# Two-block transformer on one core: compression inputs in two places, gates' activations grouped, products beside the first attention steps

## The chip, the cores and the metric

The kernel runs on one NeuronCore of a Trainium2 chip. The metric is the device time of one execution in microseconds (us). The engines named are TensorE (PE, with its weight loads as PEld), VectorE (DVE), ScalarE (ACT), GpSimd (POOL) and the queue that issues the DMAs (SP).

## What is computed

Two transformer blocks over 512 tokens of width 1024, all in float32. The first has forget-gate attention and differential attention side by side and then a mixture of 32 experts. The change lies mostly in the second block's mixer, which in the reference, cut to what matters, is:

```python
def compress_blocks(kv, pos, w1, w2):           # for the keys and for the values
    blocks = jnp.concatenate([c[:, :, :-1], c[:, :, 1:]], axis=3) + pos    # 31 windows of 32 tokens
    hid = jax.nn.silu(blocks.reshape(B, H, -1, CMP_BLOCK * DH) @ w1)       # (2048 -> 256)
    return hid @ w2                                                        # (256 -> 64)

# sparse attention, 8 heads in 2 groups, 4 query blocks of 128: over the compressed keys,
# over the selected blocks and over a window; the three are gated and added
o = gc[..., 0:1] * o_c + gc[..., 1:2] * o_s + gc[..., 2:3] * o_w

qk = silu(causal_depthwise_conv(concatenate([mq, mk]), conv_w, conv_b))    # width 4
hm = mlstm_chunkwise(mq, mk, mv, mi + bias, log_sigmoid(mf + bias))        # 4 heads
y = concatenate([y_nsa, sigmoid(mo) * normed(hm)]) @ w_out
```

## The kernel before

It is one program with a list of instructions for each engine, written stage by stage; every wait is on a semaphore that another engine's finished instruction raises. An engine takes its instructions strictly in the order written. There is no planner: the order is made by hand with generators. Dense products are done as three matmuls on split float32 (a high and a low part): ScalarE casts the high part of a weight piece (`se_lead_to`, L601), VectorE subtracts the low part (`ve_lead_to`, L590). All matmuls are recorded under the helper line L525.

The stages around the change, in order:

- **Projection** (`pe_project_nsa`, `ve_project_nsa`, `se_project_nsa`, from L2365). TensorE makes gate rows, keys and values, and then for kv = 0 (keys) and 1 (values) the compression: for two halves of the output over 16 slices each (64 recorded matmuls), with a stationary operand of 128 columns and 62 moving columns (`cmp`), a Silu on ScalarE into `hc` and a second product (`cmp2`). VectorE adds the positions to the windows and writes them to `XC` (`windows(kv)`, L2423). `XC` and `hc` have one place each, so the windows of kv = 1 wait for the `cmp` products of kv = 0, and stand behind the copy of the first `cmp2` (L2446). The stage ends with small transposes (`gat`, `mcol`) and an exponential (L2485).
- **Sparse attention** (`pe_nsa`, `ve_nsa`, `se_nsa`, from L2552): 36 units, for each of 4 head pairs first the compressed scores (branch 0, all four query blocks) and then 8 units of rising width (query block i, two branches). Step s does, per engine: TensorE the scores of unit s (A), the transposes of unit s-2 (C), beats, the values of unit s-3 (E); VectorE the normalisation of unit s-1 (N), bias and maxima of unit s (B), beats; ScalarE the copies of transposed scores (C), the exponential of unit s (B), beats. A **beat** is half a chunk (12 products of 512 columns) of the convolution's projection `mqk`, or a chunk (24 of 256) of the values' projection `mv`, with what the other engines do for it (`beside`, L648). `nsa_beats` (L2523) spreads 16 beats evenly over 36 steps: the first at step 2, then 4, 6, 8, 11, 13, 15, 17, 20, 22 and so on. The convolution c (`se_conv`, L2491, and `ve_conv`) copies its chunk to `cv` on ScalarE, and VectorE applies four taps (L2515, L2517). From c = 1 on, ScalarE puts the Silu of c-1 in front of that copy; the Silu of c = 3 stands at the first chunk of `mv`, in front of the next cast. Each Silu needs another activation table than the exponentials beside it.
- **mLSTM** (`pe_ml`, `ve_ml`, `se_ml`, from L2764): 16 units. For each head TensorE spreads a row over 128 partitions (`pe_row`, L1005): the stationary operand is 128 columns of a selector, loaded by DMA, which picks row h. ScalarE copies it (L1015), GpSimd masks it (L1021), ScalarE takes exponentials (L2834, L2835), VectorE multiplies with the scores. Beats make the output gates `og` in four chunks, each with a Sigmoid in its own place (`se_ogate`, L2809). TensorE enters the stage when all engines have ended the one before and the selector is there; SP issues the selector's DMA after these ends (`sp_ml`, L2738).

The first block's forget-gate attention uses the same `pe_row` with 8 heads and a selector of its own.

## Time and profile before

| | us |
|---|---|
| median of 3 runs | 1991.56 (1991.16 to 1992.77) |
| the profiled execution | 1991.63 |
| its span | 1989.8 |
| TensorE busy | 1778.8 (89%) |
| VectorE busy | 741.1 (37%) |
| ScalarE busy | 641.7 (32%) |
| GpSimd busy | 171.7 (9%) |

The page of the profile puts 49% of the chain that ended last on TensorE and 19% on DMA; the latter is 18% weights of the experts. The projection's end lies at about 1092 to 1122 us of the span, the sparse attention from there to 1289.7, the mLSTM up to about 1376. A busy time says how long an engine had an instruction under way; the figure in brackets behind a row of the timeline is how long the engine stood idle before it, and for whom. PEclk is the granted share of TensorE's full clock.

### The profile page before, as it was taken

The numbers are of one execution on the slowest core, as the hardware profiler recorded it, in microseconds if no ns is written. First come the engines' busy times: TensorE is split into PE (matmuls) and PEld (weight loads), VectorE is DVE, ScalarE is ACT, GpSimd is POOL, SyncE is SP. The second block draws the span as 40 slices with busy tenths as digits, with TensorE's granted clock in tenths as the row PEclk, the third lists the DMA queues.
The fourth block names the chain that finished last, engine by engine and source line by source line (L and its number), as shares of the span: only waits on it lengthen the run. The fifth ranks groups of instructions, "written<-read, shape, count | busy, mean of one in ns | idle before, by whom it ended". The sixth has DMA issues, their size and how long they took to land.

```text
span 1989.8 us, 22296 instructions
## 1 busy us (share of the span) xinstructions
PE 1778.8 (89%) x9148; PEld 1271.7 (64%) x9148; DVE 741.1 (37%) x1551; ACT 641.7 (32%) x1079; POOL 171.7 (9%) x134
## 2 busy tenths in 40 slices
PE   7999899996898888888849877898999999999998
PEld 6878566885333333333348755766888788888886
DVE  4454443455111111211164455554463452232313
ACT  3433465423010100010044255464432452122223
POOL 1000000131111111111010000011010110000111
PEclk9999899997998989899969688996999999999999
DMA  7412100357799999999934111012241122322211
GB/s 265 146 45 83 43 22 22 112 201 285 272 398 415 413 409 401 410 405 413 386 133 159 43 61 62 15 50 96 85 162 50 54 95 85 117 74 106 86 62 43
DMA packets 78445, 337.60 MB, mean 170 GB/s; under 512 B 7892, under 2 KB 15700, under 8 KB 65409
## 3 DMA queue, kind: packets, MB, share of 16 engines
q1 hardware_dynamic: 73216, 327.70, 42.7%
q0 software_dynamic: 5120, 8.40, 1.3%
q8 instruction: 75, 1.23, 0.3%
q14 instruction: 34, 0.27, 0.0%
HBM read 327.69 MB, written 16.78 MB: 173 GB/s over the span
## 4 chain that ended last, share of the span: by engine, by line
PE 49%; DMA 19%; DVE 7%; ACT 4%; issue 2%; POOL 0%; SPq 0%; POOLq 0%; DVEq 0%; ACTq 0%
PE ps L525 47%; DMA otf<-in_w 18%; DVE splitr L590 1%; ACT splitr L601 1%; DVE arenaf L2662 1%; ACT arenaf L2709 1%; PE ps L2582 1%; DVE xf L2159 1%; PE ps L772 1%; DVE otf L2517 0%; DVE xf L2967 0%; ACT hr L792 0%; PE ps L936 0%; DVE arenaf L2680 0%; DMA yd<-junk,idx 0%
## 5 line engine op out<-in xcount | busy, mean ns | idle before, releaser
L525 PE MATMUL ps<-hr,splitr 128*128 128x512 f32 (+1 forms) x2784 | 587.9, 371 | 15.0 <-issue 5.7
L525 PEld LDWEIGHTS ps<-hr,splitr 128*128 128x128 f32 x2784 | 482.8, 196 | 98.5 <-issue 14.9
L525 PE MATMUL ps<-splitr,hr 128*128 128x512 f32 (+1 forms) x1488 | 278.8, 349 | 0.0
L525 PEld LDWEIGHTS ps<-splitr,hr 128*128 128x128 f32 x1488 | 240.0, 194 | 33.6 <-issue 1.4
L590 DVE TENSOR_TENSOR splitr<-ring,splitr 128x2048 fp32r<-128x2048 f32 x63 | 145.8, 2316 | 212.2 <-ACT splitr L601 212.1
L525 PE MATMUL ps<-ring,arenaf 128*64 128x512 f32 x352 | 175.5, 657 | 20.6 <-DMA ring<-in_w 20.6
L601 ACT CAST splitr<-ring 128x2048 fp32r<-128x2048 f32 x63 | 119.9, 1904 | 161.5 <-PE ps L525 157.8
L525 PE MATMUL ps<-arenaf 128*64 128x128 f32 (+10 forms) x770 | 122.0, 365 | 28.3 <-DVE cells L2662 9.4
L1906 DVE TENSOR_TENSOR arenaf<-arenaf,ps 64x512 f32<-64x512 f32 x32 | 21.8, 681 | 328.2 <-ACT arenaf L1901 328.2
L1901 ACT ACTIVATE arenaf<-ps 64x512 f32<-64x512 f32 x32 | 19.0, 593 | 325.4 <-PE ps L525 325.4
L590 DVE TENSOR_TENSOR splitr<-arenaf,splitr 128x2048 fp32r<-128x2048 f32 x29 | 69.5, 2397 | 129.5 <-ACT splitr L601 129.5
L525 PE MATMUL ps<-splitf,arenaf 128*64 128x512 f32 x320 | 81.2, 665 | 26.8 <-DMA splitf<-in_w 26.8
L525 PEld LDWEIGHTS ps<-arenaf 128*64 128x64 f32 (+3 forms) x770 | 68.7, 171 | 54.1 <-issue 31.0
L525 PE MATMUL ps<-otf,arenaf 128*64 128x512 f32 x176 | 83.5, 631 | 19.7 <-DMA otf<-in_w 19.7
L525 PEld LDWEIGHTS ps<-ring,arenaf 128*64 128x64 f32 x352 | 50.9, 150 | 67.7 <-issue 67.6
L525 PE MATMUL ps<-splitr,otr 128*128 128x512 f32 x384 | 89.7, 392 | 1.5 <-DVE arenaf L3367 1.2
L525 PE MATMUL ps<-hf,arenaf 128*64 128x512 f32 x160 | 83.2, 681 | 0.0
L525 PEld LDWEIGHTS ps<-splitr,otr 128*128 128x128 f32 x384 | 71.5, 188 | 16.9 <-DVE arenaf L3367 1.5
L525 PE MATMUL ps<-arenaf,tq 128*64 128x512 f32 x336 | 76.7, 598 | 0.0
L601 ACT CAST splitr<-arenaf 128x2048 fp32r<-128x2048 f32 x29 | 55.2, 1903 | 59.6 <-PE ps L525 59.6
L525 PEld LDWEIGHTS ps<-splitf,arenaf 128*64 128x64 f32 x320 | 27.0, 153 | 73.3 <-issue 73.2
L926 ACT ACTIVATE arenaf<-arenaf,cells 128x128 f32<-128x128 f32 (+3 forms) x64 | 36.0, 562 | 117.5 <-DVE cells L920 117.4
(365 smaller groups left out, 2000.0 us busy)
## 6 DMA issues: line engine op xcount, KB each, us to landing
ring<-in_w SPq DMA_DIRECT2D x22, 2048.0 KB, 35.7
arenaf<-in_w SPq DMA_DIRECT2D x22, 2048.0 KB, 40.1
splitf<-in_w SPq DMA_DIRECT2D x21, 2048.0 KB, 35.5
hf<-in_w SPq DMA_DIRECT2D x20, 2048.0 KB, 35.2
ring<-in_w_in SPq DMA_DIRECT2D x11, 2048.0 KB, 11.2
otf<-in_w SPq DMA_DIRECT2D x11, 2048.0 KB, 39.5
ring<-in_w_gate_up SPq DMA_DIRECT2D x6, 2048.0 KB, 7.8
arenaf<-in_w_in SPq DMA_DIRECT2D x4, 2048.0 KB, 14.6
```

The lines of the kernel that those rows point to most:

```text
L525: return te.matmul(out, lhsT, rhs, start=start, stop=stop)
L590: ve.tensor_tensor(lo, loaded(e)[:, ks, cs], hi.bitcast(F32), ALU.subtract).then_inc(*ve_done("weights low", ("low", n), *([("entry used", ...
L601: se.copy(hi, loaded(e)[:, ks, cs]).then_inc(*se_done("weights high", ("high", n)))
L772: it = te.transpose(ps[:, 128 * k:128 * k + 128], scaled(nm, t)[:, 128 * kk:128 * kk + 128], ident)
L926: se.activation(sc[:, 0:n], sc[:, 0:n], ACT.Exp, bias=cell[:, 3:4], accum_out=cell[:, 4:5]).then_inc(*se_done("powers", ("exp",) + key))
L1901: se.activation(GATE, bank("up", b)[CAP:2 * CAP, :], ACT.Silu).then_inc(*se_done("gates", ("silu", b)))
L1906: ve.tensor_tensor(HROW, GATE, bank("up", b)[0:CAP, :], ALU.mult).then_inc(*ve_done("hidden", ("hid", b), ("free", "up", b)))
L2159: vstep(ve.scalar_tensor_tensor(X3[:, t, :], G2[:, t, 1024 * k:1024 * k + 1024], W8[:, 4 * k + t, :], X3[:, t, :], ALU.mult, ALU.add), *([ ...
L2582: it = te.transpose(ps[:, 128 * m:128 * m + 128], sc[k][:, o:o + 128], ident)
L2662: step = ve.tensor_tensor_reduce(out=sc[k], in0=bank("ns", u, k)[:, 0:n], in1=U[p % 2][:, k, 512 - n:512], scale=1.0, scalar=NEG, op0=ALU. ...
L2709: it = se.activation(sc[k], sc[k], ACT.Exp, bias=cell[:, 2 + k:3 + k], accum_out=cell[:, 4 + k:5 + k])
```

## The change

Five edits:

- `XC` and `hc` get a second place. VectorE makes the windows of kv = 1 right after those of kv = 0 and two copies of keys, before the gate rows; the copy of a row (`r_m`) and a memset (`vC4`) move up too, and the second weight piece of `mqk` is led before either `cmp2` copy. TensorE does all `cmp` products first and then both `cmp2`.
- The Silus of the convolutions 0 to 2 move from in front of the copies to the place of the fourth: four in a row at the first chunk of `mv`.
- `nsa_beats` gives one beat each at steps 0 and 1, and the other 14 over the next 34 steps: steps 4, 6, 9, 11, 14, 16, 18, 21, 23 and so on.
- The row products take as stationary operand one column of the identity, repeated 128 times by a step of zero; both selectors and their DMAs go, and the entry of the mLSTM on TensorE waits for the row, the Silus' results and the kept values, and not for the ends of the other engines.
- The output gates are copied chunk by chunk, and one Sigmoid over 2048 columns follows the fourth copy.

```diff
-        sel = carve(11264, 1024)[0:8, :]
-        XC = junk[:, 1024:1024 + 16 * 62]
-        XC4 = XC.rearrange("p (j g c) -> p j g c", j=16, g=2)
-        XCv = XC.rearrange("p (j n) -> p j n", j=16)
-        hc = thirds(OT[:, 512:640], 2)
+        XC = [a[:, 0:16 * 62] for a in (junk[:, 1024:2048], sr_[:, 2048:3072])]
+        XC4 = [a.rearrange("p (j g c) -> p j g c", j=16, g=2) for a in XC]
+        XCv = [a.rearrange("p (j n) -> p j n", j=16) for a in XC]
+        hc = [thirds(OT[:, 512 + 128 * kv:640 + 128 * kv], 2) for kv in range(2)]
-        selm = carve(6144, 512)[0:4, :]
...
-            def pe_row(key, h, rsel, row, after):
+            def pe_row(key, h, row, heads):
                 ps = take("row", key, h)
-                for w in pe_at(*after):
-                    te.wait_ge(*w)
-                mm(ps[:, :], rsel[:, 128 * h:128 * h + 128], row, True, True).then_inc(
+                mm(ps[:, :], ident[0:heads, h:h + 1].broadcast_to([heads, 128]), row, True, True).then_inc(
                     *pe_done("rows", ("row", key, h)))
...
-                sp.dma_start(sel, io["sel"]).then_inc(*sp_done("selectors", ("sel",), by=16))
...
# pe_project_nsa
-                            it = mm(ps[:, 0:62], W[:, j, 128 * m:128 * m + 128], XCv[:, j, :], j == 0, j == 15)
+                            it = mm(ps[:, 0:62], W[:, j, 128 * m:128 * m + 128], XCv[kv][:, j, :], j == 0, j == 15)
                         it.then_inc(*pe_done("products", ("cmp", kv, m), *([("entry used", e)] if m else [])))
+                for kv in range(2):
                     ps = take("cmp2", kv)
...
# ve_project_nsa
                 windows(0)
                 key_evacs(ve, ve_at, ve_done, 0, 4, kW)
+                windows(1)
                 ve_gate_rows()
+                vstep(ve.tensor_copy(r_m, r_a), ("m row",))
+                vstep(ve.memset(vC4, 0.0))
                 value_evacs(ve, ve_at, ve_done, 0)
-                ve_lead_to(jobs["mqk"][0])
+                ve_lead_to(jobs["mqk"][1])
                 for kv in range(2):
-                    if kv:
-                        windows(1)
-                        vstep(ve.tensor_copy(r_m, r_a), ("m row",))
-                        ve_lead_to(jobs["mqk"][1])
-                        vstep(ve.memset(vC4, 0.0))
                     for w in ve_at(("cmp2", kv)):
...
# se_project_nsa
-                        for w in se_at(("cmp", kv, m), *([("cmp2", 0)] if kv else [])):
+                        for w in se_at(("cmp", kv, m)):
...
             def se_conv(c):
                 for w in se_at(("prod", "mqk", c), *([("conv", c - 1)] if c else [])):
                     se.wait_ge(*w)
-                if c:
-                    se_conv_gate(c - 1)
                 se.copy(cv[:, 3:515], bank("mqk", c)[:, :]).then_inc(
...
             def se_values(c):
                 if c == 0:
-                    se_conv_gate(3)
+                    for n in range(4):
+                        se_conv_gate(n)
                 se_keep("mv", by_columns(mv))(c)
...
             def nsa_beats(s):
-                return share(16, 36, s)
+                return 1 if s < 2 else share(14, 34, s - 2)
...
# sp_ml
-                sp.dma_start(selm, io["sel"][0:4, 0:512]).then_inc(*sp_done("selectors 2", ("selm",), by=16))
# pe_ml
-                for w in pe_at(*S.ends("nsa"), ("m row",), ("selm",), ("mcol0",)):
+                for w in pe_at(("m row",), *[("qk", c) for c in range(4)], *kept("mv", 8)):
                     te.wait_ge(*w)
...
             def se_ogate(c):
                 for w in se_at(("prod", "og", c)):
                     se.wait_ge(*w)
-                se.activation(ogT[:, c, :], bank("og", c)[:, :], ACT.Sigmoid).then_inc(
-                    *se_done("gates", ("gate m", c), ("free", "og", c)))
+                it = se.copy(ogT[:, c, :], bank("og", c)[:, :])
+                if c < 3:
+                    it.then_inc(*se_done("scalar copies", ("free", "og", c)))
+                    return
+                sstep(it, ("free", "og", c))
+                se.activation(ogT, ogT, ACT.Sigmoid).then_inc(
+                    *se_done("gates", *[("gate m", n) for n in range(4)]))
```

## Rows read from the trace of the kernel before

**Rows 1.** Busy time by stretch: length, busy us of each engine (instructions), granted clock, DMA

```profile
1092.00:1122.00 30.00, 24.30 (x157) 23.67 (x155) 9.48 (x16) 7.66 (x11) 0.00 (x0) 0.65 0.12 40
1122.00:1289.70 167.70, 138.16 (x1032) 103.94 (x1032) 94.72 (x324) 85.62 (x209) 0.00 (x0) 0.87 0.12 42
1289.70:1376.00 86.30, 74.57 (x297) 51.61 (x297) 41.10 (x136) 45.78 (x77) 8.34 (x6) 0.81 0.11 37
```

**Rows 2.** Timeline, projection's end: start, us, engine, line, operation, shape, count, [idle before]

```profile
1092.34 7.25 PE L525 MATMUL ps<-junk,arenaf 128*128 128x62 f32 x64
...
1100.45 0.82 DVE L2446 COPY tq<-ps 64x31 f32<-64x31 f32 x4 [3.35 <-PE ps L525]
1101.30 1.99 DVE L2423 TENSOR_TENSOR junk<-junk,par 128x496 f32<-128x496 f32 x2
...
1103.43 13.89 PE L525 MATMUL ps<-junk,ring 128*128 128x62 f32 x64 [3.02 <-DVE junk L2423]
...
1117.73 1.03 PE L525 MATMUL ps<-otf 128*31 128x64 f32 x8 [0.40 <-ACT otf L2481]
...
1122.04 1.92 PE L525 MATMUL ps<-tq,arenaf 64*128 64x31 f32 x16 [1.91 <-ACT mcol L2485]
```

**Rows 3.** Busy time and granted clock in two short stretches of the projection

```profile
1092.00:1098.00 6.00, 6.00 (x57) 6.00 (x55) 2.29 (x1) 3.73 (x5) 0.00 (x0) 1.00 0.00 0
...
1110.00:1117.00 7.00, 7.00 (x35) 7.00 (x34) 0.00 (x0) 0.22 (x1) 0.00 (x0) 0.50 0.00 0
```

**Rows 4.** VectorE's waits, 1122 to 1290: line, waited for, us in total, times, longest

```profile
DVE cells L2677 <- ACT arenaf L2709: 31.6, 24, 2.0
DVE otf L2515 <- ACT tq L2496: 12.6, 4, 3.9
DVE splitr L590 <- ACT splitr L601: 10.2, 3, 4.7
DVE arenaf L2620 <- PE ps L525: 3.7, 3, 1.8
DVE arenaf L2662 <- PE ps L525: 3.0, 4, 1.1
```

**Rows 5.** Timeline, first steps of the sparse attention

```profile
1123.74 1.23 PE L525 MATMUL ps<-arenaf 64*128 64x128 f32 x8
...
1127.55 0.28 DVE L2662 CUSTOM_DVE_ANT_0 arenaf<-ps,arenaf 128x128 f32<-128x128 f32 x1
...
1128.09 4.68 PE L525 MATMUL ps<-hr,splitr 128*128 128x512 f32 x12
...
1129.92 0.28 DVE L2662 CUSTOM_DVE_ANT_0 arenaf<-ps,arenaf 128x128 f32<-128x128 f32 x1
...
1135.56 3.00 PE L525 MATMUL ps<-hr,splitr 128*128 128x512 f32 x12
```

**Rows 6.** Timeline, ScalarE at the second convolution

```profile
1166.80 1.28 ACT L2502 ACT_TABLE_LOAD   x1
...
1168.10 0.72 ACT L2502 ACTIVATE otf<-otf,par 128x512 f32<-128x512 f32 x1
1168.73 0.56 ACT L2496 COPY tq<-ps 128x512 f32<-128x512 f32 x1
...
1174.07 1.28 ACT L2709 ACT_TABLE_LOAD   x1
```

**Rows 7.** Timeline, from the attention's last copy to the first row product

```profile
1289.26 0.38 ACT L747 COPY otf<-ps 128x256 f32<-128x256 f32 x1
...
1291.36 1.27 PE L525 MATMUL ps<-junk,arenaf 4*128 4x512 f32 x2 [2.61 <-DMA arenaf<-in_sel]
```

**Rows 8.** Timeline, mLSTM: a cast of 2048 columns, the last gate, TensorE's stall

```profile
1296.38 1.88 ACT L601 CAST splitr<-ring 128x2048 fp32r<-128x2048 f32 x1
...
1337.09 0.60 ACT L2812 ACTIVATE arenaf<-ps 128x512 f32<-128x512 f32 x1
...
1346.45 0.90 PE L936 MATMUL ps<-con,arenaf 128*128 128x128 f32 x3 [3.57 <-DVE arenaf L987]
```

More of the change, by code:

```diff
@@ L1362, in pe_fox @@
                 tick = ticker(HEADS, lambda what, h: pe_head(h, "d", what))
-                for w in pe_at(*S.ends("diff"), ("sel",), ("frow",), *kept("fq"), *kept("fk")):
+                for w in pe_at(*S.ends("diff"), ("frow",), *kept("fq"), *kept("fk")):
                     te.wait_ge(*w)
@@ L1374, in pe_fox @@
                         if i == 0:
-                            pe_row("f", h, sel, frow, ())
+                            pe_row("f", h, frow, 8)
                         ps = take("fs", u)
@@ L2386, in pe_project_nsa @@
                         for m in range(2):
-                            it = mm(ps[0:64, 0:62], cw2[:, m, :], hc[:, m, 0:62], m == 0, m == 1)
+                            it = mm(ps[0:64, 0:62], cw2[:, m, :], hc[0][:, m, 0:62], m == 0, m == 1)
                     else:
@@ L2390, in pe_project_nsa @@
                             for m in range(2):
-                                it = mm(ps[0:31, 64 * g:64 * g + 64], hc[:, m, 31 * g:31 * g + 31], cw2[:, 2 + m, :],
+                                it = mm(ps[0:31, 64 * g:64 * g + 64], hc[1][:, m, 31 * g:31 * g + 31], cw2[:, 2 + m, :],
                                         m == 0, m == 1)
@@ L2418, in windows @@
                     pos = par[:, pa0:pa0 + 16].rearrange("p (j o) -> p j o", o=1).broadcast_to([128, 16, 31])
-                    for w in ve_at((f"two{kv}", 0), (f"two{kv}", 1), *([("cmp", 0, 1)] if kv else [])):
+                    for w in ve_at((f"two{kv}", 0), (f"two{kv}", 1)):
                         ve.wait_ge(*w)
@@ L2422, in windows @@
                         src = bass.AP(T2[kv].tensor, T2[kv][:, g, :].offset, [T2[kv].ap[0], [1, 16], [8, 31]])
-                        ve.tensor_tensor(XC4[:, :, g, :], src, pos, ALU.add).then_inc(
+                        ve.tensor_tensor(XC4[kv][:, :, g, :], src, pos, ALU.add).then_inc(
                             *ve_done("windows", ("xc", kv, g)))
@@ L2478, in se_project_nsa @@
                     for m in range(2):
-                        for w in se_at(("cmp", kv, m), *([("cmp2", 0)] if kv else [])):
+                        for w in se_at(("cmp", kv, m)):
                             se.wait_ge(*w)
-                        se.activation(hc[:, m, 0:62], bank("cmp", kv, m)[:, 0:62], ACT.Silu).then_inc(
+                        se.activation(hc[kv][:, m, 0:62], bank("cmp", kv, m)[:, 0:62], ACT.Silu).then_inc(
                             *se_done("gates", ("hc", kv, m), ("free", "cmp", kv, m)))
@@ L2778, in pe_ml @@
                         if i == 0:
-                            pe_row("m", h, selm, r_m, ())
+                            pe_row("m", h, r_m, 4)
                         ps = take("ms", u)
```

## The prediction, made before the changed kernel ran

> **What bounds the kernel now.** The change touches three stages of the second block and leaves the rest alone, so I read busy time and clock by stretch first [rows 1]: the end of the projection (30 us, TensorE busy 24.3 and at 0.65 of its clock), the sparse attention (167.7 us, busy 138.2, 0.87) and the mLSTM (86.3 us, 0.81). TensorE is busy in most of each, but who waits last differs.
>
> In the projection the timeline [rows 2] shows TensorE as the path, with one hole. The first compression (64 narrow products, 7.25 us) ends at 1099.6. A short second product, its copy on VectorE (L2446, 0.82 us) and only then the windows of the values (L2423, 1.99 us) must pass before the second compression starts at 1103.43. It has the same 64 products and takes 13.89 us, because the granted clock fell from 1.00 to 0.50 meanwhile and stayed there [rows 3] (the two levels, 2.4 and 1.2 GHz).
>
> In the sparse attention the waits of VectorE [rows 4] say that TensorE is not the bound: VectorE waits 31.6 us for ScalarE's exponentials, 12.6 us for ScalarE's copy in front of a convolution, and for TensorE only 3.7 + 3.0 us. Within a step VectorE normalises step s-1 before it biases step s, so bias, exponential and normalisation follow one another: a chain over two engines that TensorE mostly waits for. What lies on this chain counts in full; TensorE's own work counts only where it delays a score that VectorE wants.
>
> In the mLSTM TensorE works without a hole from its first row to about 1337, then the chain of row, mask, exponential and normalisation comes last and TensorE stands still for 3.57 us [rows 8].
>
> The profiled execution took 1991.63 us (span 1989.8 and 1.8 around it), 0.07 above the median of 1991.56, so its terms can be taken off the median.
>
> **Part 1, two places for the compression inputs.** The windows of the values move in front of the gate rows on VectorE and need no product any more. They end near 1084.5 (the engine is delayed by 2.0 us there, plus 0.9 for the row copy and the memset that move too, and the values' copies behind them free banks that TensorE takes only after the compressions: nothing). The weights were issued at 1075 and land in about 9 us, before 1092. So the second compression follows at 1099.6 and not at 1103.43. At full clock it takes 7.25 us as its twin did, and ends at 1106.8 instead of 1117.3. The first small second product, now behind it, takes about 0.4, while ScalarE does the last Silu; the last product starts at about 1107.4, not 1117.73, and the tail up to the attention's first product (1117.73 to 1122.04, 4.3 us) stays. Gain 10.3 us. Of these 3.8 are the hole and 6.6 are clock.
>
> Does the clock stay? The row shows that full speed lasted through the 7.25 us of these narrow products, and fell only after the hole began; I take it that it lasts through 14.5 us of them. It does not prove it: the products at 0.50 ran back to back for 13.89 us and did not bring the clock back, so they count as little work. The Trainium skill (TensorE: Matmul & The Clock Gate, The HAM clock gate) says that the clock follows how busy the engine has recently been. By that rule alone the full clock holds; but an engine busy for 13.89 us at 0.50 speaks against reading it as busy time alone.
>
> If it falls regardless, say at 1101 where the hole now is, some 13 of the 64 products run before that and 51 at the slow 217 ns (13.89/64), 11.1 us. They end at 1112.1, the small product takes 0.8, and the last one starts at 1112.9 in place of 1117.73: gain 4.8.
>
> **Part 2, the Silus of the convolution at one place.** Before, each of the convolutions 1 to 3 has on ScalarE a table load (1.28), a Silu and only then the copy that VectorE waits for [rows 6]: from 1166.80 to 1168.73, 1.93 us on the chain, because VectorE had been idle since 1165.9. Three times: 5.8 us. The exponentials need their table back; behind convolution 1 this reload (1174.07, 1.28 us) ends 0.8 us after the maxima of that step are ready, elsewhere VectorE's convolution (4 operations, 2.8 us) or a split of weights hides it. Gain 0.8. Against it: the four Silus now stand together where the fourth stood, in front of a cast of weights that VectorE waits for (L590 waits 10.2 us for three such casts [rows 4]). Three Silus more at 0.63 to 0.72 are 1.9 us. Net gain 4.7 us, bounds 2.8 (a third of the gain hidden otherwise) and 6.6 (the three Silus hidden). The copies need no table: in [rows 6] one follows a Silu at once.
>
> The skill (ScalarE: Activation LUTs, What ACT_TABLE_LOAD costs) adds some 1.38 us of drain to each load. The trace has the Silu 1.30 us after the start of its load, so I see no such drain here. With it the three loads in front of the copies would give 4.1 us more, 1971.9 in all.
>
> **Part 3, products beside the first steps.** The schedule puts half a chunk of the convolution's projection (12 products) behind the first and the second score step, the others fall one or two steps earlier. TensorE had a hole of 2.8 us there, so it looks free, but the scores of step 1 now queue behind 12 products and those of step 2 behind 24. At half clock 12 take 4.68 us, at full 3.00 [rows 5]. The first scores take 1.9 us. VectorE takes up step 1 at 1127.55, 5.5 us after the stage's first product; the scores would be there after 1.9 + 4.7 + 0.6 = 7.2. Step 2 was taken up after 7.9 us; it would be ready after 10.6 (clock back during the first twelve) to 12.3. The chain loses 2.7 to 4.4 us and gets back 1.37 that it waited for TensorE at steps 3 and 5. Cost 1.5 us taken, bounds 3.0 and, if the stage starts at full clock, a gain of 1.4. Later the beats change only who waits: TensorE's stalls shrink or grow, the chain is the same. Convolutions 1 and 3 fall beside the compressed steps, where TensorE has most work. Of the remaining 5.3 us of waits for TensorE [rows 4] I take 1.0 back, as it is at half clock less often.
>
> **Part 4, start of the mLSTM.** Its first row product waited for the selector's DMA, issued once all engines had ended the stage. Now the last thing it needs is ScalarE's copy of the values at 1289.26 (0.38 us), so it starts at about 1289.7 and not at 1291.36 [rows 7]. TensorE is the path: gain 1.65. The hole shrinks from 2.6 to 1.0 us, so the clock may not fall, which it did at 1292: 12 products took 5.25 us where 3.00 are possible, worth up to 3.3; around the hole stand products of few rows, so I take 1.0. The row product with a repeated column as stationary operand is nowhere in the trace. The nearest is the present one, 1.27 us for both passes. I take no difference; bounds 0 (it can't stream fewer columns) and 3.5 (a load of 0.3 us twice as long at 12 heads). The selector loads that vanish were beside others.
>
> **Part 5, one Sigmoid.** Three of four places lose two table loads, 7.7 us of ScalarE, but TensorE runs without a hole there: nothing. At the fourth a copy (0.58), a load, a Sigmoid of 2048 columns and the reload stand where load, Sigmoid of 512 (0.60) and reload stood. A cast of 2048 columns takes 1.88 [rows 8]; so 1.9 us more in front of the exponentials and of the last row's copy. About 0.3 of it is idle time; the chain that ends TensorE's 3.57 us of stall becomes 1.6 us later. Cost 1.6, bounds 0 (ScalarE arrives earlier by what the third place lost) and 2.5.
>
> **Sum.** -10.3 - 4.7 + 1.5 - 1.0 - 1.65 - 1.0 + 1.6 = -15.6: 1991.6 - 15.6 = 1976.0 us.
>
> **The rivals.**
> A. The clock falls in the narrow products anyway. For: they could not raise it. Against: 7.25 us at full speed. -4.8 in place of -10.3: 1981.5.
> B. More than the sum: the clock also holds at the mLSTM's start (2.3 more), the opening beats cost nothing (1.5 to 2.9) and the Sigmoid is hidden (1.6): 1976.0 - 2.3 - 1.5 - 1.6 = 1970.6.
> C. The work isn't saved, only moved: the part 1 gain is there, but the chain of the attention waits for TensorE whatever it saves. Against: only 6.7 of 167.7 us are such waits. With A and the worst bounds of parts 3 to 5 the time is 1991.6 - 4.8 - 2.8 + 3.0 + 2.5 - 1.65 = 1987.9.
> D. Slower: the repeated column. If reading one column 128 times were slow, each of 12 heads would pay before its scores. It decides from 15.6/12 = 1.3 us a head, a doubling of the present 1.27; at 2 us a head the time is 2000. Nothing in the trace speaks for it, and nothing shows the form.
>
> **How the numbers follow.** Forecast 0.60, A 0.20, B 0.13, C 0.04, D 0.03. The range runs from 1967 (B with the upper bounds of part 2 and of the opening beats, 1.9 and 1.4 more) to 1984.5 (A with the opening beats at 3.0 and the Sigmoid at 2.5, 2.4 more, and a little). A measurement of this kernel can tell 0.2%, 4 us, from no change. C lies at the edge of that: same 0.04. D gives slower 0.03; the others faster, 0.93.
>
> **What would show it.** The second compression at about 7.3 us and clock 1.00 (or 13.9 and 0.50: rival A); one load of the Silu's table in the attention and VectorE's waits for the convolution copy near 6 us in place of 12.6; the scores of step 1 some 7 us after the stage's first product; the attention 4 to 5 us shorter; the first row product directly behind ScalarE's copy; the fourth gate place some 1.9 us longer. I'm wrong if the attention's length follows TensorE's work instead, or if a row product takes over 2 us.

## The result, and the profile after

| | before | after |
|---|---|---|
| median of 4 runs each, us | 1991.36 (1986.65 to 1992.77) | 1970.49 (1959.94 to 1974.72) |
| the profiled execution | 1991.63 | 1972.32 |
| its span | 1989.8 | 1970.4 |
| TensorE busy | 1778.8 | 1768.3 |
| ScalarE busy | 641.7 | 626.9 |

The ratio is 0.9891, 95% interval 0.9848 to 0.9934: faster, by 20.9 us between the medians, where the sum had 15.6. The 1976.0 of the forecast lies inside the interval of this first comparison, but a second series of the changed kernel (below) gave 1968.58, ratio 0.9893 [0.9874, 0.9913], which leaves it out. The direction and the range held; the gain is some 5 to 6 us larger than the sum.

Busy time by stretch in the changed kernel, as in [rows 1]: length, busy us of PE, PEld, DVE, ACT, POOL (instructions), granted clock, DMA.

```profile
1091.00:1110.00 19.00, 16.38 (x157) 16.06 (x155) 6.88 (x15) 7.66 (x11) 0.00 (x0) 1.00 0.18 59
1110.00:1269.90 159.90, 134.88 (x1032) 101.21 (x1032) 94.62 (x323) 76.97 (x203) 0.00 (x0) 0.91 0.12 45
1269.90:1356.00 86.10, 75.17 (x297) 51.40 (x297) 42.03 (x136) 39.38 (x72) 8.07 (x6) 0.80 0.11 37
```

The same 157 matmuls that took 30 us now take 19, at clock 1.00 in place of 0.65; the same 1032 of the attention take 159.9 in place of 167.7; the mLSTM is no shorter. The timeline of TensorE at the projection's end (start, us, engine, line, operation, tile, shape, count, [idle before]), against [rows 2]:

```profile
1091.12 7.25 PE L523 MATMUL ps<-junk,arenaf 128*128 128x62 f32 x64
1098.21 7.31 PE L523 MATMUL ps<-arenaf,ring 128*128 128x62 f32 x64
1105.45 1.08 PE L523 MATMUL ps<-otf 128*64 128x62 f32 x12
...
1109.95 1.25 PE L523 MATMUL ps<-tq,arenaf 64*128 64x31 f32 x16 [2.59 <-ACT mcol L2479]
```

and the granted clock over the two compressions, against [rows 3]:

```profile
1091.00:1098.00 7.00, 7.00 (x66) 7.00 (x64) 2.43 (x2) 3.74 (x5) 0.00 (x0) 1.00 0.00 0
1098.00:1105.40 7.40, 7.40 (x68) 7.38 (x67) 2.29 (x1) 2.23 (x3) 0.00 (x0) 1.00 0.00 0
```

The second compression has no idle time in front of it and takes 7.31 us, not 13.89. VectorE's waits in the attention (line, waited for: us in total, times, longest), against [rows 4]:

```profile
DVE cells L2670 <- ACT arenaf L2702: 33.1, 26, 1.6
DVE splitr L588 <- ACT splitr L599: 11.9, 3, 6.5
DVE otf L2508 <- ACT tq L2488: 5.4, 4, 1.8
DVE arenaf L2655 <- PE ps L523: 4.2, 5, 1.1
...
DVE arenaf L2613 <- PE ps L523: 1.2, 1, 1.2
```

The wait for the convolution's copy (L2508, before the change L2515) fell from 12.6 to 5.4. The wait for the casts (L588) rose by less than two: one of the three now waits 6.5 us, because in front of it stand a load and the four Silus. ScalarE there:

```profile
1202.48 1.28 ACT L2494 ACT_TABLE_LOAD   x1
1203.77 2.56 ACT L2494 ACTIVATE otf<-otf,par 128x512 f32<-128x512 f32 x4
1206.24 1.88 ACT L599 CAST splitr<-ring 128x2048 fp32r<-128x2048 f32 x1
1208.03 0.36 ACT L2711 COPY arenaf<-ps 128x256 f32<-128x256 f32 x1
1208.40 1.28 ACT L2702 ACT_TABLE_LOAD   x1
```

The start of the mLSTM and the stall that ends it, against [rows 7, 8]:

```profile
1269.96 1.09 PE L523 MATMUL ps<-junk,con 4*128 4x512 f32 x2 [1.04 <-ACT otf L745]
1270.98 1.53 PE L523 MATMUL ps<-otf 64*128 64x128 f32 x4
1272.44 5.49 PE L523 MATMUL ps<-hr,splitr 128*128 128x512 f32 x12
...
1285.81 1.12 PE L523 MATMUL ps<-junk,con 4*128 4x512 f32 x2
...
1326.25 0.90 PE L934 MATMUL ps<-con,arenaf 128*128 128x128 f32 x3 [3.10 <-DVE arenaf L985]
```

From the start of ScalarE's last copy (1269.44) to the start of the row product it is 0.52 us, in the kernel before 2.10. With the repeated column it takes 1.09 to 1.12 us.

Where the 19.4 us between the two spans lie, from marks that both traces have (the start of the first compression, of the attention's first product, of its last copy, of the first row product and of the product behind the stall, and the end):

| stretch | before | after | difference | forecast |
|---|---|---|---|---|
| up to the first compression | 1092.34 | 1091.12 | -1.22 | 0 |
| first compression to attention | 29.70 | 18.83 | -10.87 | -10.3 |
| attention | 167.22 | 159.49 | -7.73 | -4.2 |
| last copy to first row product | 2.10 | 0.52 | -1.58 | -1.65 |
| first row product to end of stall | 55.09 | 56.29 | +1.20 | +0.6 |
| the rest | 643.35 | 644.15 | +0.80 | 0 |

Two terms need an explanation: why the attention gained 3.5 us more than the sum had, and why the mLSTM became longer although its start was to be faster.

The attention can be split where VectorE takes up the scores of step 9. In both orders four beats and one convolution lie in front of that. The rows, before and after:

```profile
1159.28 0.64 DVE L2620 TENSOR_TENSOR arenaf<-ps,arenaf 128x124 f32<-128x124 f32 x2 [0.38 <-PE ps L525]
```

```profile
1146.69 0.63 DVE L2613 TENSOR_TENSOR arenaf<-ps,arenaf 128x124 f32<-128x124 f32 x2
```

That is 37.24 us after the attention's first product before the change and 36.74 after it: 0.5 us less, where the sum had 1.5 more (part 3). Behind this mark it is 129.98 and 122.75: 7.2 less, where the sum had 5.7 (4.7 of part 2 and 1.0 for the clock). So 2.0 of the 3.5 us lie in the opening and 1.5 behind it.

### The profile page after: what moved, and what is told of

Read it like the earlier page. It is cut to its first block, busy times and chain, and to the rows that moved or that the text cites. A ratio compares the mean times of both kernels' runs of the same rounds, so it can differ in the third digit from the quotient of the medians.

```text
span 1970.4 us, 22276 instructions
## 1 busy us (share of the span) xinstructions
PE 1768.3 (90%) x9148; PEld 1262.5 (64%) x9148; DVE 741.9 (38%) x1551; ACT 626.9 (32%) x1068; POOL 172.5 (9%) x134
## 4 chain that ended last, share of the span: by engine, by line
PE 48%; DMA 19%; DVE 8%; ACT 4%; issue 2%; SPq 0%; POOL 0%; POOLq 0%; DVEq 0%; ACTq 0%
PE ps L523 47%; DMA otf<-in_w 18%; DVE splitr L588 1%; ACT splitr L599 1%; ACT arenaf L2702 1%; DVE arenaf L2655 1%; DVE xf L2154 1%; PE ps L2575 1%; ACT hr L790 0%; DVE arenaf L2673 0%; PE ps L770 0%; DVE otf L2510 0%; DVE xf L2964 0%; PE ps L934 0%; DVE hr L824 0%
## 5 line engine op out<-in xcount | busy, mean ns | idle before, releaser
L523 PEld LDWEIGHTS ps<-hr,splitr 128*128 128x128 f32 x2784 | 485.2, 197 | 99.0 <-issue 14.5
L588 DVE TENSOR_TENSOR splitr<-ring,splitr 128x2048 fp32r<-128x2048 f32 x63 | 145.8, 2316 | 215.1 <-ACT splitr L599 214.9
L523 PE MATMUL ps<-arenaf 128*64 128x128 f32 (+9 forms) x754 | 110.3, 352 | 22.7 <-DVE arenaf L1737 8.7
L588 DVE TENSOR_TENSOR splitr<-arenaf,splitr 128x2048 fp32r<-128x2048 f32 x29 | 69.5, 2397 | 129.6 <-ACT splitr L599 129.6
L523 PEld LDWEIGHTS ps<-arenaf 128*64 128x64 f32 (+2 forms) x754 | 65.3, 167 | 47.2 <-issue 28.8
L523 PEld LDWEIGHTS ps<-ring,arenaf 128*64 128x64 f32 x352 | 50.5, 149 | 65.7 <-issue 65.6
```

What stands on the lines that cost most here:

```text
L523: return te.matmul(out, lhsT, rhs, start=start, stop=stop)
L588: ve.tensor_tensor(lo, loaded(e)[:, ks, cs], hi.bitcast(F32), ALU.subtract).then_inc(*ve_done("weights low", ("low", n), *([("entry used", ...
```

## The experiments

All kernels were timed in several rounds beside the kernel before on the same chip. "Theory" is what the forecast or the last reading says. The table at the end of this section gathers what the traces of all of them show.

### Each part alone

`p1_places` to `p4_rows` are the kernel before with one part of the change. Part 1 alone:

```diff
-        XC = junk[:, 1024:1024 + 16 * 62]
...
-        hc = thirds(OT[:, 512:640], 2)
+        XC = [a[:, 0:16 * 62] for a in (junk[:, 1024:2048], sr_[:, 2048:3072])]
...
+        hc = [thirds(OT[:, 512 + 128 * kv:640 + 128 * kv], 2) for kv in range(2)]
...
                 key_evacs(ve, ve_at, ve_done, 0, 4, kW)
+                windows(1)
...
+                for kv in range(2):
                     ps = take("cmp2", kv)
```

> The kernel before with part 1 alone (two places for the compression inputs and results). Theory (the hole and the clock are both gone): the second compression takes 7.3 us, the stretch from the first compression's start to the attention's first product falls from 29.7 to about 18.9 us, the time by 10.8. Rival (what the change gained there needs the other parts, or the clock falls when the attention still opens with a hole): the stretch falls by 5 at most. The attention and the mLSTM stay within 1.5 us of 167.2 and 55.1.

Measured: 1978.85 us against 1990.88 (ratio 0.9942 [0.9923, 0.9961]); from the first compression to the attention 18.83 us, to the hundredth what the whole change gives. The attention behind it was 168.43 us, no shorter. It began at full clock, but the granted clock was 0.50 again from 1110.8 to 1121.0, so its opening ran at half clock for about as long as in the kernel before (1122.0 to 1131.7). Part 1 does what was worked out.

Part 2 alone:

```diff
             def se_conv(c):
...
-                if c:
-                    se_conv_gate(c - 1)
...
             def se_values(c):
                 if c == 0:
-                    se_conv_gate(3)
+                    for n in range(4):
+                        se_conv_gate(n)
```

> The kernel before with part 2 alone (four Silus at one place). Theory (the chain over VectorE and ScalarE): three copies are ready 1.93 us earlier, one reload 0.8, the four Silus cost 1.9: attention 4.7 us shorter than 167.2, the time 4.7 less. Rival (the clock joins in: shorter stalls keep TensorE at full clock): 7 to 8 us. Rival (TensorE is the bound): under 2 us.

Measured: 1983.10 us, ratio 0.9968 [0.9957, 0.9979]; the attention 159.59 us, 7.6 shorter. The time alone can't tell 4.7 from 7.6 (the interval is 4.2 to 8.6 us), so the trace has to. VectorE's waits in this kernel:

```profile
DVE cells L2676 <- ACT arenaf L2708: 30.8, 24, 1.6
DVE splitr L590 <- ACT splitr L601: 12.1, 3, 6.5
DVE otf L2514 <- ACT tq L2494: 6.5, 4, 1.8
DVE arenaf L2619 <- PE ps L525: 2.6, 3, 1.8
...
DVE arenaf L2661 <- PE ps L525: 1.6, 3, 1.1
```

The kernel before had one more row for TensorE than [rows 4] show, so its waits for TensorE are 3.7 + 3.0 + 2.1 = 8.8 us (here there is the same row of 2.1 for L2685):

```profile
DVE arenaf L2686 <- PE ps L525: 2.1, 1, 2.1
```

For ScalarE: copies -6.1, exponentials -0.8, casts +1.9, in all -5.0. That is the forecast's own sum (5.8 + 0.8 - 1.9 = 4.7), each term met to 0.3. The rest, 2.5 us, are waits for TensorE, that fell from 8.8 to 6.3, while TensorE's clock rose from 0.87 to 0.92. That agrees with the rival (the clock joins in), added to the theory's 5 us. Most of the 2.5 us, 2.2, lie in two waits of the kernel before, 1.49 us at 1206.9 and 1.10 us at 1277.1. In front of each lies a stretch at clock 0.50 (1193.2 to 1203.4 and 1268.3 to 1275.1). With part 2 alone that first stretch is 3.4 us long (from 1194.1) and the wait behind it 0.39; in place of the second the clock is 1.00 throughout, and there is no wait.

Part 3 alone:

```diff
-                return share(16, 36, s)
+                return 1 if s < 2 else share(14, 34, s - 2)
```

> The kernel before with part 3 alone (beats at steps 0 and 1). Theory (the chain): the scores of the first steps come later, little is got back, attention 0 to 2 us longer than 167.2. Rival (the hole of 2.8 us is filled and convolutions fall beside steps with much TensorE work): 3 us shorter.

Measured: 1986.23 us, ratio 0.9982 [0.9972, 0.9992]; the attention 165.91 us, 1.3 shorter than before and 1.9 to 2.5 shorter than in the three other traces with the same order there (table below). The theory had it 0 to 2 longer; this points towards the rival.

Part 4 alone:

```diff
-                mm(ps[:, :], rsel[:, 128 * h:128 * h + 128], row, True, True).then_inc(
+                mm(ps[:, :], ident[0:heads, h:h + 1].broadcast_to([heads, 128]), row, True, True).then_inc(
...
-                for w in pe_at(*S.ends("nsa"), ("m row",), ("selm",), ("mcol0",)):
+                for w in pe_at(("m row",), *[("qk", c) for c in range(4)], *kept("mv", 8)):
```

> The kernel before with part 4 alone (repeated identity column, no wait for the ends of the stage). Theory: a row product takes as long as before (1.1 us at full clock), the gap from ScalarE's last copy to the first row falls from 2.1 to 0.5 us, the time by 1.6, less than can be told. Rival (clock holds at the entry too): 4 to 5 us.

Measured: 1989.84 us, ratio 0.9992 [0.9977, 1.0006]; copy to row product 0.52 us in place of 2.10, as in the changed kernel. In the time the 1.6 us can't be told from nothing. Each row product took 1.09 to 1.12 us: the repeated column costs nothing.

Part 5 alone, run after the others:

```diff
-                se.activation(ogT[:, c, :], bank("og", c)[:, :], ACT.Sigmoid).then_inc(
-                    *se_done("gates", ("gate m", c), ("free", "og", c)))
+                it = se.copy(ogT[:, c, :], bank("og", c)[:, :])
+                if c < 3:
+                    it.then_inc(*se_done("scalar copies", ("free", "og", c)))
+                    return
+                sstep(it, ("free", "og", c))
+                se.activation(ogT, ogT, ACT.Sigmoid).then_inc(
+                    *se_done("gates", *[("gate m", n) for n in range(4)]))
```

> The kernel before the change with part 5 alone: the output gates copied chunk by chunk and one Sigmoid of 2048 columns behind the fourth copy. From the second row product of the mLSTM to the end of TensorE's stall the kernels with four Sigmoids took 39.24 to 39.25 us (before the change, parts 1, 3 and 4 alone, the changed kernel with part 5 undone) and those with one 40.44 to 40.45. Theory: 40.4 here too, part 5 costs 1.2 us of the 1.6 forecast and the time is 0.06% longer, within what can be measured. Rival: it is the other parts together with the one Sigmoid that cost it: 39.3.

Measured: 1989.24 us against 1990.55, ratio 0.9995 [0.9982, 1.0008]; from the second row product to the end of the stall 40.44 us, where the kernel before has 39.24. So the one Sigmoid does cost 1.2 us, which the time can't show.

### The hole and the clock

Was it the hole that cost the clock? In `u1_long_hole` the changed kernel gets it back by an added wait; the windows are ready all the same. The keys' small second product also stands between the two compressions again, so the kernel to compare it with is `u1_small_hole` below, which has the same order without the wait.

```diff
                 for kv in range(2):
...
+                        for w in pe_at(*([("low", jobs["mqk"][1])] if kv else [])):
+                            te.wait_ge(*w)
...
-                for kv in range(2):
                     ps = take("cmp2", kv)
```

> The changed kernel, but the second compression's 64 products must wait until VectorE has made the low part of the first weight piece of mqk, so that TensorE stands idle between the two compressions, by some 3.9 us as it did before the change; the windows of the values stay in their own place and are ready. Theory: the idle time itself cost the clock, so the second compression takes 13.9 us at 0.50 again and the stretch from the first compression's start to the attention's first product grows from 18.8 to about 29 us (3.9 for the hole and 6.6 for the clock); the time is some 10 us longer than the changed kernel's, close to 1981. Rival: the clock fell for something else before the change (the place of the window on VectorE, the DMAs), and only the hole is paid: about 22.7 us, time some 4 us longer. Third: the clock falls inside the second compression, so only part of the 6.6 is lost: between 24 and 28 us.

Measured: 1980.13 us against 1990.18, ratio 0.9947 [0.9928, 0.9965]. TensorE's timeline in this kernel, and the clock in the second compression:

```profile
1091.06 7.25 PE L523 MATMUL ps<-junk,arenaf 128*128 128x62 f32 x64
1098.71 0.41 PE L523 MATMUL ps<-otf 128*64 128x62 f32 x4 [0.41 <-ACT otf L2476]
1102.89 13.89 PE L523 MATMUL ps<-arenaf,ring 128*128 128x62 f32 x64 [3.76 <-DVE tq L2441]
```

```profile
1104.00:1116.00 12.00, 12.00 (x58) 12.00 (x57) 0.00 (x0) 0.22 (x1) 0.00 (x0) 0.50 0.00 0
```

3.76 us of idle time, and the 64 products take 13.89 us again, to the hundredth the figure of [rows 2]. From the first compression to the attention it is 30.43 us: the gain of part 1 is gone. In `u1_small_hole` it is 19.58 us. So the cause is shown: the one wait costs 10.85 us, both the hole and the clock.

`u1_small_hole` has the same order without the added wait, which leaves a hole of 0.41 us between the compressions and another behind the second.

> The changed kernel, but the keys' short second product stands between the two compressions again, which leaves TensorE a hole of about 0.4 us for ScalarE's Silu, while the rest of part 1 stays. Theory: so short a hole doesn't cost the clock: the second compression stays at 7.3 us and the stretch from the first compression's start to the attention's first product is 19.2 to 19.8 us in place of 18.8, the time the same within 0.1%. Rival: any hole among these narrow products lets the clock fall: 25 us or more, and the time some 6 us longer.

Measured: 1963.67 us, ratio 0.9873 [0.9850, 0.9896].

```profile
1091.68 7.25 PE L523 MATMUL ps<-junk,arenaf 128*128 128x62 f32 x64
1099.34 0.41 PE L523 MATMUL ps<-otf 128*64 128x62 f32 x4 [0.41 <-ACT otf L2474]
1099.69 7.36 PE L523 MATMUL ps<-arenaf,ring 128*128 128x62 f32 x64
```

Short holes leave the clock alone; the stretch is 19.58 us, 0.75 more than without them. That the whole time came out 7 us under the changed kernel's first median is no merit of the edit: the table at the end shows where such amounts come from.

### The steps and the Sigmoids, undone

`u3_beats` is the changed kernel with `share(16, 36, s)` again.

> The changed kernel, but with the sixteen beats spread evenly over the 36 steps as before the change (part 3 undone). Done alone, part 3 made the attention 1.3 us shorter; done together with part 2 it seemed to add nothing (159.5 us with both, 159.6 with part 2 alone). Theory: the two don't add, since part 2 had taken the same waits for TensorE already: attention 159.5 within 0.6 us, the time the same. Rival 1: part 3 is worth its 1.3 us here too: attention 160.8. Rival 2: its first steps cost (1.1 us seen at step 2 in the trace of part 3 alone) and nothing is got back: attention 1 to 1.5 us shorter without it.

Measured: 1968.72 us, ratio 0.9895 [0.9877, 0.9913]; the attention 157.84 us, 1.65 shorter than with part 3. So alone part 3 shortened the attention and beside part 2 it doesn't; rival 2 is nearest. VectorE takes up step 9 after 35.94 us here and after 36.74 in the changed kernel, so 0.8 of the 1.65 us lie in the opening. Its first steps cost what their timeline said: VectorE takes up the scores of step 1 after 6.05 us and those of step 2 after 9.42, with even beats after 4.75 and 7.13.

`u5_sigmoid` is the changed kernel with the four Sigmoids at their places again (the reverse of the diff of part 5).

> The changed kernel, but with the four Sigmoids of the output gates each at its own place, as before the change (part 5 undone). Part 4 alone made the stretch from the mLSTM's first row product to the end of TensorE's stall 53.55 us; the changed kernel, with part 5 as well, takes 56.29. Theory: the one Sigmoid in front of the exponentials costs those 2.7 us: stretch 53.6, the time 2.7 us (0.14%) shorter than the changed kernel's. Rival 1: the sum's term of 1.6 us is right and the rest comes from the clock at the stage's start: stretch 54.7. Rival 2: the Sigmoid is hidden and something of the other parts made the stage longer: stretch 56.3, no difference.

Measured: 1967.97 us, ratio 0.9895 [0.9877, 0.9914]; from the first row product to the end of the stall 55.04 us. None of the three numbers was hit, because the stretch has two halves that must be read apart. Up to the second row product it is 15.79 us, as in the changed kernel (15.85); from there 39.25, against 40.44. The one Sigmoid costs 1.2 us, and the rest is in the first half.

ScalarE at the fourth place of the output gates, first in the changed kernel, then with four Sigmoids:

```profile
1314.29 0.58 ACT L2804 COPY arenaf<-ps 128x512 f32<-128x512 f32 x1
1314.89 1.28 ACT L2809 ACT_TABLE_LOAD   x1
1316.18 1.91 ACT L2809 ACTIVATE arenaf<-arenaf 128x2048 f32<-128x2048 f32 x1
1318.11 1.28 ACT L2831 ACT_TABLE_LOAD   x1
```

```profile
1312.49 1.28 ACT L2804 ACT_TABLE_LOAD   x1
1313.78 0.60 ACT L2804 ACTIVATE arenaf<-ps 128x512 f32<-128x512 f32 x1
1314.40 1.28 ACT L2826 ACT_TABLE_LOAD   x1
```

5.1 us against 3.2: 1.9 more, as forecast; 0.7 of it does not reach the end of the stall.

### The changed kernel again, and two versions of it

`after_again` is the changed kernel unaltered, to see what no edit does.

> The changed kernel once more, unaltered, beside the other three of this call. It tells how much of a difference between two executions belongs to no edit: VectorE's order of work in the attention should be the same to a hundredth of a microsecond but for the steps that wait for TensorE, and the attention's length and the time from the mLSTM's first row product to its second (15.9, 15.8, 15.8, 14.3 and 12.7 us in five kernels with the same list there) should move by the clock alone, in jumps of about 1.6 us. If instead both stay at 159.5 and 15.85, the differences seen belonged to the edits.

Measured: 1968.58 us (1962.42 to 1970.61), ratio 0.9893 [0.9874, 0.9913]. Attention 159.66 us; from the first row product to the second 14.29, not 15.85, though nothing was changed: one of the jumps of 1.6 us.

In `u2_cast_first` the Silus stand behind the cast that VectorE waits for:

```diff
             def se_values(c):
-                if c == 0:
-                    for n in range(4):
-                        se_conv_gate(n)
...
             def se_nsa():
-                beats = beside(se_lead, ("mqk", se_conv, 4, 2), ("mv", se_values, 8, 1))
+                def lead(p):
+                    se_lead(p)
+                    if p == jobs["mv"][0]:
+                        for n in range(4):
+                            se_conv_gate(n)
+                beats = beside(lead, ("mqk", se_conv, 4, 2), ("mv", se_values, 8, 1))
```

> The changed kernel, with the four Silus of the convolution one place later on ScalarE: behind the cast of 2048 columns that VectorE waits for, and no longer in front of it. In the changed kernel VectorE waited 6.5 us for that cast, of which the table load and the four Silus are 3.8. Theory: that wait falls to 2.7, and 1.4 of it comes back since the reload of the exponentials' table ends 1.4 us later than the step's maxima; the attention is 2.4 us shorter (157.1 to 157.7 at the same clock) and the time 2 to 3 us shorter. Rival 1: all 3.8 are given back, since the exponentials come next on the same chain: no difference. Rival 2: the step's scores wait for TensorE then, whose beat was hidden under the 6.5 us: gain 1 or less, VectorE's wait for TensorE larger by what is missing.

Measured: 1962.50 us (1958.75 to 1971.85), ratio 0.9880 [0.9857, 0.9903]; the attention 157.74 us, 1.8 and 1.9 shorter than in the changed kernel's two traces. VectorE in this kernel:

```profile
1202.79 2.29 DVE L588 TENSOR_TENSOR splitr<-ring,splitr 128x2048 fp32r<-128x2048 f32 x1 [2.63 <-ACT splitr L599]
1209.33 0.17 DVE L2667 RECIPROCAL cells<-cells 128x2 f32<-128x2 f32 x1 [2.51 <-ACT arenaf L2704]
```

The wait for the cast is 2.63 in place of 6.50, as expected; the next exponentials are later and all waits for them 34.5 in place of 33.1 (the 1.4 expected). Net -2.5 for ScalarE; waits for TensorE gave back 0.9 of it (7.0 against 6.1).

`v_best` has this, the four Sigmoids and the even beats.

> The changed kernel with three alterations: the Silus behind the cast, four Sigmoids at their own places again, and the beats spread evenly as before the change. Worked out from the separate readings: Silus -2.4, Sigmoids -1.2, beats -1.6 (the trace with even beats had an attention of 157.84 us in place of 159.49): 5.2 us shorter than the changed kernel, about 1965. Rival 1: the beats are worth nothing on average, what was seen was the clock: 3.6 shorter. Rival 2: the gains don't add, as those of part 2 and part 3 did not: 2 or less.

Measured: 1965.81 us (1965.43 to 1967.46), ratio 0.9884 [0.9863, 0.9905]. The attention is the shortest of all, 156.58, and the half behind the second row product 39.26. In time it is 2.8 us under the changed kernel beside it, with ranges that overlap, and not under `u2_cast_first`. Both have the lower medians in that series and the shorter stages in their traces; that either beats the changed kernel in time is not shown.

### All traces side by side

All attentions have the same 1032 matmuls and 94.6 to 94.7 us of VectorE's work. The columns: length of the attention; VectorE's waits in it for ScalarE and for TensorE (sums of rounded rows, good to 0.1); TensorE's granted clock; from the mLSTM's first row product to the second, and from there to the end of the stall; the rest of the span, behind that stall, where no edit has an instruction.

| kernel | attention | for ACT | for PE | clock | row 1 to 2 | to end of stall | rest |
|---|---|---|---|---|---|---|---|
| before | 167.22 | 58.1 | 8.8 | 0.87 | 15.85 | 39.24 | 643.4 |
| p1_places | 168.43 | 58.1 | 10.0 | 0.86 | 15.82 | 39.24 | 643.4 |
| p4_rows | 167.80 | 58.1 | 9.4 | 0.88 | 14.30 | 39.25 | 644.7 |
| p5_sigmoid | 167.98 | 58.0 | 9.8 | 0.88 | 15.81 | 40.44 | 638.9 |
| p3_beats | 165.91 | 57.3 | 8.3 | 0.88 | 15.86 | 39.25 | 643.4 |
| p2_silus | 159.59 | 53.1 | 6.3 | 0.92 | 14.29 | 40.91 | 640.5 |
| u3_beats | 157.84 | 53.1 | 4.6 | 0.92 | 14.28 | 40.45 | 644.1 |
| after | 159.49 | 53.1 | 6.1 | 0.91 | 15.85 | 40.44 | 644.2 |
| after_again | 159.66 | 53.1 | 6.2 | 0.90 | 14.29 | 41.05 | 640.4 |
| u1_long_hole | 160.26 | 53.1 | 6.8 | 0.91 | 15.79 | 40.45 | 644.3 |
| u1_small_hole | 160.07 | 53.1 | 6.8 | 0.91 | 12.70 | 40.45 | 637.1 |
| u5_sigmoid | 159.58 | 53.1 | 6.1 | 0.91 | 15.79 | 39.25 | 640.4 |
| u2_cast_first | 157.74 | 50.6 | 7.0 | 0.91 | 12.70 | 40.45 | 637.2 |
| v_best | 156.58 | 50.5 | 5.9 | 0.92 | 14.28 | 39.26 | 643.2 |

The column of waits for ScalarE is the cleanest: it follows the order of ScalarE's work, 57.3 to 58.1 without part 2, 53.1 with it, 50.5 or 50.6 with the cast first. The waits for TensorE are lower and its clock higher in every kernel with part 2 than in every kernel without it; within either group one doesn't order the other. The last column varies by 7.6 us over traces, with no edit that explains it, and the start of the first compression lies between 1088.8 and 1093.2.

## Why the prediction was right, point by point

**The bounds.** The reading held that the projection was TensorE's, the attention the chain of VectorE and ScalarE. The first is shown by part 1 alone, whose 10.9 us are in the stretch worked out for it. The second is shown by part 2: taking 5.0 us of waits for ScalarE away shortened the attention by all of that. Rival C (work moved only) is out. The prediction counted 6.7 us of waits for TensorE; with the row of L2686 there were 8.8, so what the clock could give back was larger than it read.

**Part 1, -10.3.** Measured -10.87. The assumption that carried 6.6 of it, that full speed lasts through 14.5 us of narrow products, held, and the run with the long hole shows the other side of it: with 3.76 us of idle time it doesn't. Rival A is out. The missing half microsecond: both small products run together behind the second compression, as one group of 1.08 us from 1105.45 (14.33 us after the first compression's start, where the sum had 15.06 for the last of them).

**Part 2, -4.7.** The terms were right, 5.0 measured for ScalarE. The Trainium skill (ScalarE: Activation LUTs, What ACT_TABLE_LOAD costs) puts a drain of some 1.38 us beside each load; the load of 1202.48 is followed by its Silu at 1203.77, 1.29 us later, and the waits for ScalarE fell by 5.0 and not by 9. The trace doesn't agree with a drain of that size here.

**Which terms were mis-sized.** Two terms carry nearly all of the 3.5 us that the attention gained beyond the sum.

The larger is part 3's +1.5 for the opening. Up to step 9 the changed kernel was 0.5 us quicker than the kernel before in its first trace (36.74 against 37.24) and 0.1 slower in its second (37.36). Two things are in this. The order of the beats costs 0.8 us up to step 9 with part 2 (36.74 against 35.94 in `u3_beats`; 37.84 in `u2_cast_first` against 37.07 in `v_best`) and 0.2 without it (37.48 in `p3_beats`). The clock can give back more: `u3_beats` and part 2 alone have the same order of beats and Silus, but in the first the clock was at 0.50 for 6.8 us of the opening (1110.6 to 1117.4), in the second for 9.7 us (from the stage's start at 1122.9), and step 9 came after 35.94 and 37.31 us. A full clock at the entry alone is no guarantee of that: part 1 alone had it, lost it after 0.7 us, and took up step 9 after 38.44 us. The forecast had bounded this term by 3.0 and a gain of 1.4, so the measured -0.5 and +0.1 lie inside its bounds.

The other is the -1.0 for fewer waits for TensorE at half clock. Behind step 9 these waits fell from 5.1 us to 2.9 in the changed kernel and to 2.7 with part 2 alone: 2.3 and 2.5 less. Over the whole stage all kernels with part 2 have 4.6 to 7.0 where those without have 8.3 to 10.0, with 0.90 to 0.92 of the clock in place of 0.86 to 0.88. The forecast saw the link and gave it one number without a row behind it. That a shorter chain leaves TensorE less idle, and so less at half clock, is a reading and is not shown: no run separated the clock from the order of the steps, and idle time in total doesn't order the clock. TensorE is idle for 26.2 us of the attention with part 3 alone and for 26.6 with part 2 alone, at clock 0.88 and 0.92.

**Part 3, +1.5 cost.** The mechanism is there: step 1 is taken up at 6.05 us and step 2 at 9.42 (forecast 7.2 and 10.6 to 12.3, before 5.51 and 7.88), less late than forecast. In this trace the stage starts at full clock (the first 16 products take 1.25 us, before 1.92); but in the second trace it starts at half clock (1.92), and the two steps come after 6.65 and 10.03 us, still earlier than forecast. Over the stage its price depends on what stands beside it: 1.3 to 2.5 us shorter alone, 1.2 to 1.8 us longer beside part 2 (159.49 and 159.66 against 157.84; 157.74 against 156.58), except that part 2 alone, with even beats too, has 159.59. The prediction said that later beats only change who waits. In the changed kernel that agrees with the waits (53.1 for ScalarE with either order); alone, the part took 0.8 us of waits for ScalarE and 0.5 to 1.7 for TensorE away. Of what it costs beside part 2, 0.8 us lie up to step 9, as said. Why it gains alone, and so why the two parts don't add, stays open, at a size of one to two microseconds.

**Part 4, -1.65 and -1.0.** The first half is right to 0.07 us in all kernels with the part. Rival D is out: 1.09 to 1.12 us a row product in the mLSTM, where 1.3 more a head were needed, and the eight of the first block take the same as before (1.09, 2.07 and six times 1.12 us, in both kernels). The -1.0 for the clock was a mean of two outcomes, not a term: the first 12 dense products took 5.49 us in one trace of the changed kernel and 4.30 in the other, and the first half of the stretch 15.85 and 14.29. As a mean it did come out: the nine traces with part 4 have 14.44 us for that half on average and the five without it 15.53, 1.1 more, though both groups hold values near 14.3 and 15.8.

**Part 5, +1.6.** Measured +1.20 in every trace but two (40.44 or 40.45 against 39.24 to 39.26). The two are the changed kernel's second trace (41.05, one Sigmoid) and part 2 alone (40.91, four): in both the last row product took 2.07 us in place of 1.12, so there TensorE was at half clock in front of the stall. That three of four places gain nothing held as well.

**The range and the rivals.** The median fell nearest to rival B's 1970.6, but not for its reasons: the clock did not hold at the mLSTM's start in the profiled run, and the Sigmoid was not hidden. What B had right is the cheap opening. The rest of the distance, 1976.0 to 1970.5, is the attention (3.5 us), half a microsecond of part 1 and what belongs to no edit. That the median came so near to B's number is luck.

## What to carry to other kernels

A hole on TensorE can cost more than its own length, where the clock falls in it and what follows doesn't bring it back: here 3.8 us of waiting for a single buffer cost 10.9, and giving the buffer a second place brought back both. Activations that need another table belong where no copy waits behind them; and if they must stand in front of something, behind the cast that VectorE waits for is better than in front of it (3.9 us of wait, of which 2.5 stayed). Price edits of a microsecond by the same stretch in several traces, split at marks that separate what the clock does from what the order does: the whole time moved by 5 us and more without an edit.

## What the runs showed of the hardware

- The narrow products kept the clock, but did not raise it: 128 of them with 128x62 ran at 1.00 for 14.4 us; 64 of them ran back to back at 0.50 for 13.89 us and stayed there, in the kernel before, in part 5 alone (13.88) and with the long hole. The Trainium skill (TensorE: Matmul & The Clock Gate, The HAM clock gate) has the clock follow recent activity; by busy time alone these 13.89 us should have brought it back, and the rows don't agree with that.
- A hole of 0.41 us in front of 0.4 us of small products left the clock at full speed; one of 3.76 us behind them took it. In the kernel before the clock fell at 1101.0, 0.6 us into the hole of 3.02 us, with the long hole at 1102.6, 3.4 us into it; so these rows give no length from which a hole costs the clock.
- After the hole at the mLSTM's start, the same instructions up to the second row product took 12.70, 14.28 to 14.30 or 15.79 to 15.86 us in fourteen traces, nothing between, and the changed kernel itself had two of these values. The first 12 dense products there took 3.01, 4.28 to 4.61 and 5.21 to 5.49 us. How much of this stretch is at half clock thus differs between executions, in steps of 1.6 us.
- A stationary operand read with a step of zero (one column, 128 times) is as fast as 128 stored columns: 1.12 us for both passes of 512 columns.
